# A transformer block in fp32 on one core: the stages of the first phase reordered, the gate stores moved to another DMA queue, and six homes in place of four for the adaLN tiles

## The chip, the cores and the metric

The kernel runs on one core of a Trainium2 chip. Its time is the device time of one execution, in microseconds. The engines are named as the profile names them: PE (matrix multiply, with its weight loads as PEld), DVE (vector), ACT (scalar), POOL (idle here) and SP, which only issues DMAs.

## The reference

One block of batch 1, 256 tokens and width 2048, all in float32. With `mod = silu(c) @ w_ada + b_ada`, cut into nine rows of 2048 (`sh1, sc1, gt1, ... gt3`):

```python
u = modulate(rmsnorm(h, g1), sh1, sc1)
h = h + 0.5 * gt1 * ((silu(u @ w_in_a) * (u @ w_in_b)) @ w_out)      # 2048 -> 2 x 5632 -> 2048
u = modulate(rmsnorm(h, g2), sh2, sc2)
h = h + gt2 * hybrid_mixer(u)     # one wide projection, windowed attention, mLSTM, gates, w_out
u = modulate(rmsnorm(h, g3), sh3, sc3)
h = h + 0.5 * gt3 * swiglu(u, ffn2)
out = rmsnorm(h, final_g)
```

## The kernel before

**Products.** Each fp32 product is made of three in fp32r: ACT rounds a weight block to `hi` (L1452), DVE subtracts to get `lo` (L2040), and PE adds act_hi\*hi, act_lo\*hi and act_hi\*lo. A *chunk* is 1 MB of weights (128x2048); it has two *units*. A unit is 12 matmuls of 512 columns. `raw` holds four chunks and `hi` four units, so SP may load chunk n only when PE is through with chunk n-4, and ACT may round unit n only when PE is through with unit n-4. All engines run their instructions in program order.

**adaLN.** `w_ada` (laid out as 144 blocks of 128 x 2048) is not multiplied on PE. DVE multiplies its tiles by `cond_row` and sums them, one after another. At the start these are 32 *start tiles* of 1 MB (L2069, `start_tile`): tiles 2kt and 2kt+1 give scale and shift of the 128 features kt, without which neither `act_hi` (L1709) nor `act_lo` (L2090) of that kt exists. Later they are tiles of 0.5 MB (L2057, `ada`), which land in a ring of four homes in `ada_w`. The tiles of the attention phase ("gates") have two homes of their own in `gate_w`. `ada_plan` says with which chunk a tile is loaded and used. SP waits for the last tile in a home to be used before it loads the next one there, and everything behind that on SP waits too.

**The first phase** (`first_body`, 36 chunks, 72 units counted from 0) runs the first FFN's input product before all of kt is known. The list `STAGES` sets which kt of which column blocks come in which order. One stage uses the four pairs of PSUM banks `pa, pb` and `px, pq`; when the next stage needs other column blocks, ACT copies the sums out to `part` (L1719) and, where the new block had been begun, copies them back (L1722). `MOVES` lists these copies; `todo` says in which unit ACT issues them. `tile_unit(k)` says before which unit DVE handles start tile k, `load_before(k)` before which chunk SP loads it.

**Gate rows.** `store_gate` (L680) writes a row of `mod` (gt1, gt2, gt3) from SBUF to DRAM as 2048 single elements of 4 bytes; `load_gate` (L686) reads it back broadcast over the partitions. All DMAs but five small ones are issued by SP, on queue q1. The five of ACT go on queue q10.

**After the first phase** come, for each FFN, three input phases (`ffn1_in0..2`) and three output phases (`ffn1_out0..2`). Between them lie `proj`, `rest` (4 chunks of 264 columns) and `gates` (with the attention and mLSTM heads), and `up` and `wout`. Before an output phase can end its first block, the last hidden block has to be multiplied (DVE L2185), turned (DVE L2171, ACT L1463) and split (ACT L1486, DVE L2178).

Of the kernel before, what the change touches and what calls it, by code (L numbers as in the profile page):

```python
# [33 lines left out]
P = 128  # L34
NC = 512
RING = 4
ADA_RING = 4
# [10 lines left out]


GROUPS = 6  # L50
STAGES = [(0, ((0,), (1,))), (1, ((0, 1),)), (2, ((0, 1),)),
# [3 lines left out]
LEFT = range(12, 16)  # L55
# [26 lines left out]
def build(nc, x, x_t, c, cols, positions, w_ada, w_first, ffn1_w_in, ffn1_w_out, w_proj, w_rest, w_gates,  # L82
# [3 lines left out]
    KD = D // P  # L86
# [93 lines left out]
    for cidx in sorted(tiles_at):  # L180
        for t in tiles_at[cidx]:
            load_at.setdefault(cidx + (AHEAD if t in gates_tiles else 0), []).append(t)
    ring_of = {}
    for ring in (gates_tiles, [t for t in range(len(TILES)) if t not in gates_tiles]):
        size = 2 if ring is gates_tiles else ADA_RING
        for k, t in enumerate(ring):
            ring_of[t] = (ring is gates_tiles, k % size, k // size, ring[k - size] if k >= size else None)

    MODS = [(GT1, 3)] + [(m, 1) for m in (SH2, SC2, GT2, SH3, SC3, GT3)]

# [22 lines left out]

    def tile_unit(k):

        return (0, 0, 1, 2)[k] if k < 4 else 3 + round(2.2 * (k - 4))

    def load_before(k):

        return k // 2 if k < 4 else tile_unit(k) // 2 + 1  # L220

    def hi_unit(kt):

# [78 lines left out]
    with ExitStack() as ctx:  # L302
# [356 lines left out]
        def _(sp):  # L659
# [14 lines left out]
                    sp.wait_ge(s_dve, k - S_RING + 1)  # L674
                sp.dma_start(start_home(k), w_ada[m * KD + kt, :, :]).then_inc(ada_s_in[k % S_RING], 16)

            def store_gate(m, done):

                sp.wait_ge(mod_ok, mod_count(m))
                sp.dma_start(gate_rows[ROWS_OUT.index(m):ROWS_OUT.index(m) + 1, :].rearrange("a (k p) -> p (a k)", p=P),  # L680
                             mod[:, m * KD:(m + 1) * KD], allow_slow_non_contiguous=True).then_inc(done, 16)

            def load_gate(row, done, landed):

                sp.wait_ge(done, 16)
# [70 lines left out]

            def load_x_again(b):

                sp.wait_ge(s_dve, 2 * KD)
                if b > 1:  # L760
                    sp.wait_ge(gated_sum, 2 * b - 2)
                sp.dma_start(gate_w[:, b % 2, :].rearrange("p (t n) -> p t n", t=TT), x[:, :, b * NC:(b + 1) * NC])\
                    .then_inc(x_again[b % 2], 16)

            def load_ffn(f):
                g0 = 0
                for p, ng in enumerate(PARTS):
                    name = f"ffn{f}_in{p}"
                    def ffn_in(i, first, name=name, g0=g0):
                        if name == "ffn1_in2" and i == 0:  # L770
                            for k in (0, 1):
                                load_x_again(k)
                        if name in PARTIAL and i < PARTIAL[name][1]:
                            for j in range(plan[name].per[i]):
                                pos = N_FIRST + 2 * (PARTIAL[name][0] + i) + j
                                load(plan[name], i, j, w_first[pos], 4)
                                load_ada(plan[name].at(i) + j)
                            return
                        if (name, i) in FAST:
                            load_fast(name, i)  # L780
                            return
                        for j in range(8):
                            if not at_seam(plan[name], i, j):
                                ffn_chunk(name, i, i + g0, j, j)
                            load_ada(plan[name].at(i) + j)
                            if name == "ffn1_in2" and (i, j) in ((1, 4), (1, 7)):
                                load_x_again(2 + (j == 7))
                            if (name, i, j) == ("ffn1_in1", 3, 3):
                                store_gate(GT1, gt1_out)
                            if (name, i, j) == ("ffn2_in0", 0, 4):  # L790
                                load_pair(0, 0)
                                load_pair(0, 1)
                            if (name, i, j) == ("ffn2_in0", 0, 7):
                                store_gate(GT3, gt3_out)
                    over(sp, ng, ffn_in)
                    name = f"ffn{f}_out{p}"
                    def ffn_out(b, first, name=name, g0=g0, ng=ng):
# [29 lines left out]
                over(sp, 4, body)  # L827

            proj_pair("proj", w_proj)
            store_gate(GT2, gt2_out)  # L830
            for j in range(4):
                load(plan["rest"], 0, j, w_rest[:, j * 4:j * 4 + 4, :], 4, REST_W)
            proj_pair("gates", w_gates)
# [596 lines left out]
        def _(act):  # L1430
# [273 lines left out]
            def first_body(ph):  # L1704
# [18 lines left out]

                todo = {}
                for k, move in enumerate(MOVES):
                    todo.setdefault(move[0] + 3, []).append(k)
                assert [k for u in sorted(todo) for k in todo[u]] == list(range(len(MOVES)))
                for u in range(N_UNITS):
                    split(ph, 0, u // 2, u % 2, 2)
# [27 lines left out]
            def partial_body(ph, i, g, last):  # L1757
# [16 lines left out]
                if last:  # L1774
                    silu(ph)(i)
                    nat_evac_at(nb - 1, i - 1)

            def rows_load(k):

                if k == 0:  # L1780
# [21 lines left out]

            def first_casts(n_):

                if n_ == 10:
                    s_casts("ffn2_in0")
                if n_ >= 12:
                    fast_cast(0, n_ - 12)

            def ffn(f, mid):  # L1810
                for p, ng in enumerate(PARTS):
                    ph = plan[f"ffn{f}_in{p}"]
                    for i in range(ng):
# [4 lines left out]
                        if (f"ffn{f}_in{p}", i) in FAST:  # L1818
                            fast_body(f"ffn{f}_in{p}", i)
                            continue  # L1820
                        in_body(ph, i, i == 0, silu(ph), None, True, mid=mid if p == 0 else None,
                                step=rows_load if (f, p, i) == (1, 2, 0) else
                                first_casts if (f, p, i) == (2, 0, 0) else None)
                        if (f, p, i) == (1, 2, 2):

# [53 lines left out]
            for n_, (j, half, k0, n) in enumerate(units(4, 4)):  # L1879
# [5 lines left out]
                    act.activation(m_st[:, 8:10, :], m_st[:, 10:12, :], ACT.Ln, bias=1.0).then_inc(g_ln, 1)  # L1885
                if n_ == 3:
                    copy_b(3)

            def qk_silu(hds):

# [1150 lines left out]
```

## Time and profile before

| | us |
|---|---|
| median of 3 runs (2038.3 to 2039.84) | 2039.84 |
| the profiled execution's own time | 2043.58 |
| its span, first to last instruction | 2041.8 |
| PE busy | 2019.9 |
| DVE busy | 1685.4 |
| ACT busy | 1206.6 |
| mean granted TensorE clock | 0.997 |

The chain that ended last is 93% PE. The profiled execution lies 3.7 us above the median, and 1.8 us of its time lie outside the span. A group of rows below shows a start time in us from the first instruction, a duration in us, engine, line, operation, names, shape and count, and in brackets the idle time of the engine just before and what ended it.

### The profile page before, as it was taken

To read this page: it belongs to the slowest core of one execution; us is meant where nothing else is said; L and a number is where in the kernel's file an instruction comes from. 1 tells how busy PE (TensorE), PEld (TensorE's weight loads), DVE (VectorE), ACT (ScalarE), POOL (GpSimd) and SP (SyncE) were. 2 spreads that over 40 slices of the span, in tenths; PEclk is the share of its full clock that TensorE was granted. 3 is DMA by queue.
4 is the path that set the end of the run, shared out by engine and by line. 5 is a ranking of instruction groups with operands and counts; after the bars stand their busy time and mean duration, and the time that the engine had idled before them with its cause. 6 is when DMAs were issued, how large, how long until landed. Compare 5 with 4: busy or idle time off the path is not lost.

```text
span 2041.8 us, 23814 instructions
## 1 busy us (share of the span) xinstructions
PE 2019.9 (99%) x9090; PEld 1662.6 (81%) x9090; DVE 1685.4 (83%) x2208; ACT 1206.6 (59%) x1658; POOL 2.4 (0%) x14
## 2 busy tenths in 40 slices
PE   8999999999999999999999999999999999999998
PEld 6788888887888888888777888888888888888887
DVE  7898698878889988788998898887777777787786
ACT  5777644655345555446555676567775577755764
POOL 0000000000000000000000000000000000000000
PEclk8999999999999999999999999999999999999999
DMA  9998799899999868976665687575565556555554
GB/s 386 393 380 310 286 346 385 329 310 372 364 357 345 311 244 347 343 278 182 221 219 209 237 304 270 184 234 179 206 229 204 192 179 210 209 199 201 173 198 150
DMA packets 102658, 544.96 MB, mean 267 GB/s; under 512 B 17424, under 2 KB 19728, under 8 KB 53776
## 3 DMA queue, kind: packets, MB, share of 16 engines
q1 hardware_dynamic: 101696, 543.30, 73.1%
q8 instruction: 72, 1.18, 0.2%
q14 instruction: 42, 0.34, 0.1%
q10 hardware_dynamic: 848, 0.14, 0.0%
HBM read 541.28 MB, written 2.12 MB: 266 GB/s over the span
## 4 chain that ended last, share of the span: by engine, by line
PE 93%; DMA 3%; DVE 2%; ACT 1%; issue 1%; SPq 0%; DVEq 0%; ACTq 0%
PE pa L934 13%; PE pb L934 13%; PE pa L942 13%; PE pb L942 12%; PE pb L938 12%; PE pa L938 12%; DMA raw<-in_ffn_w_in_dram 2%; PE pa L1028 2%; PE pa L1034 2%; PE pa L1031 2%; DMA raw<-in_w_first_dram 1%; PE pa L949 1%; PE pq L1201 1%; PE pa L1192 1%; PE pb L1201 1%; PE pa L1197 1%
## 5 line engine op out<-in xcount | busy, mean ns | idle before, releaser
L1452 ACT CAST hi<-raw 128x1024 fp32r<-128x1024 f32 (+2 forms) x662 | 679.1, 1034 | 694.9 <-PE pa L942 251.5
L2040 DVE TENSOR_TENSOR lo<-raw,hi 128x1024 fp32r<-128x1024 f32 (+2 forms) x662 | 784.6, 1201 | 277.3 <-ACT hi L1452 274.3
L2057 DVE SCALAR_TENSOR_TENSOR ada_w<-ada_w,cond_row 128x1024 f32<-128x1024 f32 x207 | 247.2, 1218 | 0.0
L934 PE MATMUL pa<-hi,act_hi 128*128 128x512 f32 x800 | 222.0, 393 | 0.0
L934 PE MATMUL pb<-hi,act_hi 128*128 128x512 f32 x800 | 217.1, 393 | 0.1
L942 PE MATMUL pb<-lo,act_hi 128*128 128x512 f32 x800 | 213.9, 389 | 0.0
L942 PE MATMUL pa<-lo,act_hi 128*128 128x512 f32 x784 | 213.6, 389 | 0.0
L938 PE MATMUL pb<-hi,act_lo 128*128 128x512 f32 x784 | 209.8, 389 | 0.0
L938 PE MATMUL pa<-hi,act_lo 128*128 128x512 f32 x720 | 196.0, 389 | 0.0
L942 PEld LDWEIGHTS pb<-lo,act_hi 128*128 128x128 f32 x800 | 150.2, 188 | 31.4
L934 PEld LDWEIGHTS pb<-hi,act_hi 128*128 128x128 f32 x800 | 148.6, 188 | 32.4 <-issue 2.2
L934 PEld LDWEIGHTS pa<-hi,act_hi 128*128 128x128 f32 x800 | 148.6, 188 | 31.8 <-issue 1.7
L938 PEld LDWEIGHTS pb<-hi,act_lo 128*128 128x128 f32 x784 | 147.2, 188 | 30.9
L942 PEld LDWEIGHTS pa<-lo,act_hi 128*128 128x128 f32 x784 | 147.2, 188 | 30.8
L938 PEld LDWEIGHTS pa<-hi,act_lo 128*128 128x128 f32 x720 | 135.2, 188 | 28.6
L1463 ACT COPY hid_t<-buf_a 32x256 f32<-32x256 f32 x240 | 97.0, 404 | 15.2 <-DVE buf_a L2171 11.9
L934 PE MATMUL pa<-hi,hid_hi 128*128 128x512 f32 x376 | 103.8, 391 | 1.6 <-ACT hi L1452 1.6
L942 PE MATMUL pa<-lo,hid_hi 128*128 128x512 f32 x376 | 103.3, 390 | 1.1 <-DVE lo L2040 1.1
L938 PE MATMUL pa<-hi,hid_lo 128*128 128x512 f32 x376 | 103.3, 390 | 0.0
L942 PE MATMUL pb<-lo,hid_hi 128*128 128x512 f32 x372 | 102.5, 388 | 0.0
L934 PE MATMUL pb<-hi,hid_hi 128*128 128x512 f32 x330 | 89.2, 389 | 0.0
L938 PE MATMUL pb<-hi,hid_lo 128*128 128x512 f32 x330 | 89.1, 389 | 0.0
(462 smaller groups left out, 2612.5 us busy)
## 6 DMA issues: line engine op xcount, KB each, us to landing
raw<-in_ffn_w_in_dram SPq DMA_DIRECT2D x107, 1024.0 KB, 5.1
ada_w<-in_w_ada_dram SPq DMA_DIRECT2D x207, 512.0 KB, 6.5
raw<-in_ffn_w_out_dram SPq DMA_DIRECT2D x60, 1024.0 KB, 6.8
raw<-in_w_first_dram SPq DMA_DIRECT2D x48, 1024.0 KB, 6.9
raw<-in_w_gates_dram SPq DMA_DIRECT2D x32, 1024.0 KB, 4.9
raw<-in_w_proj_dram SPq DMA_DIRECT2D x31, 1024.0 KB, 5.7
pair<-in_ffn_w_in_dram SPq DMA_DIRECT2D x20, 1024.0 KB, 6.9
raw<-in_ffn_w_out_dram SPq DMA_DIRECT2D x24, 768.0 KB, 4.6
```

Of the source, the lines that this page charges most:

```text
L934: pe.matmul(bank[:, tt, cols], a_hi[:, k0 + kk, tok], w_hi[:, kk, cols], start=start and kk == 0, stop=False, skip_group_check=on)
L938: pe.matmul(bank[:, tt, cols], a_lo[:, k0 + kk, tok], w_hi[:, kk, cols], start=False, stop=False, skip_group_check=on)
L942: mm = pe.matmul(bank[:, tt, cols], a_hi[:, k0 + kk, tok], w_lo[:, 2 * half + kk, cols], start=False, stop=stop and rest is None and kk == ...
L949: mm = pe.matmul(bank[:, tt, cols], a_lo[:, k0 + kk, tok], w_hi[:, kk, cols], start=False, stop=stop and kk == n - 1, skip_group_check=on)
L1028: pe.matmul(bank, a_hi[:, kk, :], fast_hi(o)[:, kk, :], start=start and kk == 0, stop=False, skip_group_check=True)
L1031: pe.matmul(bank, a_lo[:, kk, :], fast_hi(o)[:, kk, :], start=False, stop=False, skip_group_check=True)
L1034: mm = pe.matmul(bank, a_hi[:, kk, :], fast_lo(o)[:, kk, :], start=False, stop=kk == 1, skip_group_check=True)
L1201: mm = pe.matmul(bank(m)[:, tt, :], act_hi[:, blocks[m][0], tok], w_lo[:, s0 + m, 0:NC], start=False, stop=True, skip_group_check=True)
L1452: act.copy(hi_of(ph, i, j, half)[:, 0:n, 0:w], raw_of(ph, i, j)[:, 2 * half:2 * half + n, 0:w])\
L1463: ins = act.copy(dst, src)
L2040: dve.tensor_tensor(lo_of(ph, i, j)[:, s, 0:w], raw_of(ph, i, j)[:, s, 0:w], hi_of(ph, i, j, half)[:, 0:n, 0:w].bitcast(F32), ALU.subtract)\
L2057: dve.scalar_tensor_tensor(out=wt, in0=wt, scalar=1.0, in1=cond_row[:, half * ADA_W:(half + 1) * ADA_W], op0=ALU.mult, op1=ALU.mult, accum ...
```

## The change

Three parts. (1) In the first phase the first stage has kt 0 alone, its second stage kt 0 and then kt 1, and the sixth kt 1, 2 and 3; start tiles are handled up to two units later and loaded up to one chunk later, and ACT copies the banks of the first stage out one unit after their last use, not three. (2) The three stores of a gate row go from SP's queue to ACT's, each at a later place of the program. (3) The adaLN tiles up to the third block of `ffn1_out1` take turns in six homes: the four of `ada_w` and the two of `gate_w`. The reloads of x into `gate_w` wait for the last of them.

```diff
-STAGES = [(0, ((0,), (1,))), (1, ((0, 1),)), (2, ((0, 1),)),
-          (2, ((2,), (3,))), (1, ((2, 3),)), (0, ((2, 3),)),
+STAGES = [(0, ((0,),)), (1, ((0,), (1,))), (2, ((0, 1),)),
+          (2, ((2,), (3,))), (1, ((2, 3),)), (0, ((1, 2, 3),)),
...
+    WIDE = [t for cidx in tiles_at for t in tiles_at[cidx] if cidx < plan["ffn1_out1"].at(2) + 2]
+    ring_of, holder, turns = {}, {}, [0] * (ADA_RING + 2)
+    for ring, first_slot, size in ((WIDE, 0, ADA_RING + 2),
+                                   ([t for t in range(len(TILES)) if t not in WIDE + gates_tiles], 0, ADA_RING),
+                                   (gates_tiles, ADA_RING, 2)):
...
     def tile_unit(k):
-        return (0, 0, 1, 2)[k] if k < 4 else 3 + round(2.2 * (k - 4))
+        return (0, 0, 2, 4)[k] if k < 4 else 5 + round(2.2 * (k - 4))
     def load_before(k):
-        return k // 2 if k < 4 else tile_unit(k) // 2 + 1
+        return (0, 0, 1, 2)[k] if k < 4 else tile_unit(k) // 2 + 1
...
             def load_x_again(b):
-                sp.wait_ge(s_dve, 2 * KD)
+                sp.wait_ge(ada_done, LAST_WIDE[b % 2] + 1)
...
-                            if (name, i, j) == ("ffn1_in1", 3, 3):
-                                store_gate(GT1, gt1_out)
-                            if (name, i, j) == ("ffn2_in0", 0, 7):
-                                store_gate(GT3, gt3_out)
...
             proj_pair("proj", w_proj)
-            store_gate(GT2, gt2_out)
...
-                    todo.setdefault(move[0] + 3, []).append(k)
+                    todo.setdefault(move[0] + (1 if move[1] == 0 else 3), []).append(k)
...
+            def store_gate(m, done):
+                act.wait_ge(mod_ok, mod_count(m))
+                act.dma_start(gate_rows[ROWS_OUT.index(m):ROWS_OUT.index(m) + 1, :].rearrange("a (k p) -> p (a k)", p=P),
+                              mod[:, m * KD:(m + 1) * KD], allow_slow_non_contiguous=True).then_inc(done, 16)
+            def first_gate(n_):
+                if n_ == 8:
+                    store_gate(GT1, gt1_out)
...
             def first_casts(n_):
+                if n_ == 8:
+                    store_gate(GT3, gt3_out)
...
+                if n_ == 5:
+                    store_gate(GT2, gt2_out)
```

The first place is the start of the first phase. ACT's rows from its first rounding on, before (`act_hi` is the split input of one kt, `part<-pa` a bank copied out):

```order
L1452 CAST hi<-raw 128x1024
L1709 ACTIVATE act_hi<-n_t,mod 128x256
L1452 CAST hi<-raw 128x1024 x2
L1709 ACTIVATE act_hi<-n_t,mod 128x256
L1452 CAST hi<-raw 128x1024 x3
L1719 COPY part<-pa 128x1024
L1719 COPY part<-pb 128x1024
```

and now (L1447, L1704 and L1714 are L1452, L1709 and L1719 of before):

```order
L1447 CAST hi<-raw 128x1024
L1704 ACTIVATE act_hi<-n_t,mod 128x256
L1447 CAST hi<-raw 128x1024
L1714 COPY part<-pa 128x1024
L1714 COPY part<-pb 128x1024
L1447 CAST hi<-raw 128x1024
L1714 COPY part<-px 128x1024
L1714 COPY part<-pq 128x1024
L1447 CAST hi<-raw 128x1024 x2
L1704 ACTIVATE act_hi<-n_t,mod 128x256
```

Two pairs of copies now stand before and behind the rounding of unit 2, and the second `act_hi` comes behind unit 4 in place of unit 2. DVE's rows there, from the first `act_lo` on, before (`ada_s`, `ada_w` <- ... are start tiles 2 and 3):

```order
L2090 SCALAR_TENSOR_TENSOR act_lo<-n_t,mod,act_hi 128x256
L2040 TENSOR_TENSOR lo<-raw,hi 128x1024
L2069 SCALAR_TENSOR_TENSOR ada_s,macc<-ada_s,cond_row 128x2048
L2040 TENSOR_TENSOR lo<-raw,hi 128x1024
L2069 SCALAR_TENSOR_TENSOR ada_w,macc<-ada_w,cond_row 128x2048
L2076 TENSOR_TENSOR mod<-macc,cols_in 128x1
L2077 SCALAR_TENSOR_TENSOR gain<-macc,sc_bias,cols_in 128x1
L2084 SCALAR_TENSOR_TENSOR n_t<-n_t,gain,rs_row 128x256
L2090 SCALAR_TENSOR_TENSOR act_lo<-n_t,mod,act_hi 128x256
L2040 TENSOR_TENSOR lo<-raw,hi 128x1024
```

and now (L2051, L2080 and L2101 are L2040, L2069 and L2090 of before):

```order
L2101 SCALAR_TENSOR_TENSOR act_lo<-n_t,mod,act_hi 128x256
L2051 TENSOR_TENSOR lo<-raw,hi 128x1024 x2
L2080 SCALAR_TENSOR_TENSOR ada_s,macc<-ada_s,cond_row 128x2048
L2051 TENSOR_TENSOR lo<-raw,hi 128x1024 x2
L2080 SCALAR_TENSOR_TENSOR ada_w,macc<-ada_w,cond_row 128x2048
L2087 TENSOR_TENSOR mod<-macc,cols_in 128x1
L2088 SCALAR_TENSOR_TENSOR gain<-macc,sc_bias,cols_in 128x1
L2095 SCALAR_TENSOR_TENSOR n_t<-n_t,gain,rs_row 128x256
L2101 SCALAR_TENSOR_TENSOR act_lo<-n_t,mod,act_hi 128x256
L2051 TENSOR_TENSOR lo<-raw,hi 128x1024
```

Start tile 2 has moved behind the `lo` of unit 1, and tile 3, with what makes kt 1 of it, behind the `lo` of unit 3. SP's loads there, before:

```order
L675 DMA ada_s<-in_w_ada_dram 128x2048 x2
L700 DMA raw<-in_w_first_dram 128x2048
L675 DMA ada_s<-in_w_ada_dram 128x2048
L675 DMA ada_w<-in_w_ada_dram 128x2048
L700 DMA raw<-in_w_first_dram 128x2048
L742 DMA n_t<-in_x_t_dram 128x512
L675 DMA ada_w<-in_w_ada_dram 128x2048
L700 DMA raw<-in_w_first_dram 128x2048
L675 DMA gate_w<-in_w_ada_dram 128x2048
```

and now:

```order
L681 DMA ada_s<-in_w_ada_dram 128x2048 x2
L700 DMA raw<-in_w_first_dram 128x2048
L681 DMA ada_s<-in_w_ada_dram 128x2048
L700 DMA raw<-in_w_first_dram 128x2048
L681 DMA ada_w<-in_w_ada_dram 128x2048
L700 DMA raw<-in_w_first_dram 128x2048
L742 DMA n_t<-in_x_t_dram 128x512
L681 DMA ada_w<-in_w_ada_dram 128x2048
L700 DMA raw<-in_w_first_dram 128x2048
```

The second and the third chunk of `raw` now each have one tile less ahead of them. The second place is the store of gt2. SP's rows before, at the end of `proj`:

```order
L668 DMA ada_w<-in_w_ada_dram 128x1024 [waits ada_done] x2
L700 DMA raw<-in_w_proj_dram 128x2048 [waits unit_used] x3
L680 DMA gate_rows<-mod 128x16x1 [waits mod_ok]
L700 DMA raw<-in_w_rest_dram 128x4x264 [waits unit_used] x4
L700 DMA raw<-in_w_gates_dram 128x2048 [waits unit_used] x4
```

and ACT's now, in `rest`:

```order
L1894 ACTIVATE m_st<-m_st 128x8
L1447 CAST hi<-raw 128x2x264 x2
L1861 ACTIVATE proj<-pb 128x2x512
L1447 CAST hi<-raw 128x2x264 x2
L1776 DMA gate_rows<-mod 128x16x1
L1447 CAST hi<-raw 128x2x264 x2
L1907 ACT_TABLE_LOAD
L1907 ACTIVATE proj<-proj,cols_in 128x2x128 x4
L1447 CAST hi<-raw 128x1024
```

The store no longer stands ahead of the loads of `rest` on SP; it stands on ACT behind the rounding of the sixth unit of `rest`, when SP has come to the loads of `gates`.

## Rows read from the trace of the kernel before

**Rows 1.** The page, busy time and instructions of the engines.

```profile
PE 2019.9 (99%) x9090; PEld 1662.6 (81%) x9090; DVE 1685.4 (83%) x2208; ACT 1206.6 (59%) x1658; POOL 2.4 (0%) x14
```

**Rows 2.** Windows (stretch: length, busy by engine, clock, DMA share, GB/s).

```profile
20.00:40.00 20.00, 17.05 (x62) 13.22 (x61) 18.70 (x22) 9.19 (x11) 0.00 (x0) 0.83 1.01 423
```

**Rows 3.** Timeline of PE, start of the first phase.

```profile
12.37 0.71 PE L1171 MATMUL pq<-ident,st 128*128 128x128 f32 x4 [2.70 <-DVE st L2606]
...
19.48 0.70 PE L1192 MATMUL pa<-hi,act_hi 128*128 128x512 f32 x2 [0.38 <-ACT act_hi L1709]
...
28.41 1.19 PE L1192 MATMUL pa<-hi,act_hi 128*128 128x512 f32 x2 [2.83 <-ACT act_hi L1709]
...
33.66 0.93 PE L1192 MATMUL px<-hi,act_hi 128*128 128x512 f32 x2
...
36.73 1.07 PE L1192 MATMUL pa<-hi,act_hi 128*128 128x512 f32 x4
...
39.45 1.07 PE L1192 MATMUL pb<-hi,act_hi 128*128 128x512 f32 x4
```

**Rows 4.** Timeline of PE, units 20 and 24 of the first phase.

```profile
80.25 1.16 PE L1192 MATMUL pa<-hi,act_hi 128*128 128x512 f32 x4
...
92.99 0.40 PE L1192 MATMUL pa<-hi,act_hi 128*128 128x512 f32 x1
```

**Rows 5.** Timeline of ACT, start of the first phase.

```profile
26.81 1.04 ACT L1452 CAST hi<-raw 128x1024 fp32r<-128x1024 f32 x1 [6.53 <-DMA raw<-in_w_first_dram]
27.76 0.50 ACT L1709 ACTIVATE act_hi<-n_t,mod 128x256 fp32r<-128x256 f32 x1
...
34.29 1.00 ACT L1719 COPY part<-pa 128x1024 f32<-128x1024 f32 x1
```

**Rows 6.** Timeline of DVE, start tile 3 and what follows.

```profile
24.25 2.28 DVE L2069 SCALAR_TENSOR_TENSOR ada_w<-ada_w,cond_row 128x2048 f32<-128x2048 f32 x1
...
26.90 0.48 DVE L2084 SCALAR_TENSOR_TENSOR n_t<-n_t,gain,rs_row 128x256 f32<-128x256 f32 x1
```

**Rows 7.** Windows behind two gate stores, and beside four small loads of ACT.

```profile
432.50:441.00 8.50, 8.50 (x39) 7.02 (x39) 5.88 (x10) 3.58 (x6) 0.00 (x0) 1.00 0.67 43
918.00:928.00 10.00, 10.00 (x48) 8.30 (x47) 8.93 (x17) 3.91 (x5) 0.00 (x0) 1.00 0.46 18
558.00:568.00 10.00, 10.00 (x46) 8.29 (x45) 9.66 (x13) 4.01 (x4) 0.00 (x0) 1.00 0.98 381
```

**Rows 8.** The line of the gate stores, L680.

```profile
DMA to landing us min/median/max: 15.4/15.9/16.0
```

**Rows 9.** Timelines of ACT and PE, start of `ffn1_out1`.

```profile
469.49 2.00 ACT L1452 CAST hi<-raw 128x1024 fp32r<-128x1024 f32 x2 [2.90 <-DMA raw<-in_ffn_w_out_dram]
...
475.86 3.33 ACT L1463 COPY hid_t<-buf_a 32x256 f32<-32x256 f32 x8 [1.62 <-DVE buf_a L2171]
...
485.89 1.17 PE L934 MATMUL pa<-hi,hid_hi 128*128 128x512 f32 x4 [1.57 <-ACT hi L1452]
...
489.09 1.19 PE L942 MATMUL pa<-lo,hid_hi 128*128 128x512 f32 x4 [1.11 <-DVE lo L2040]
```

**Rows 10.** Timelines of ACT and PE, second block of `ffn2_in0`.

```profile
1373.16 2.00 ACT L1452 CAST hi<-raw 128x1024 fp32r<-128x1024 f32 x2 [5.38 <-DMA raw<-in_ffn_w_in_dram]
...
1379.42 0.73 PE L1028 MATMUL pa<-hi_b,s_in 128*128 128x512 f32 x2 [1.36 <-ACT pa L1521]
```

**Rows 11.** Timelines of ACT and PE, end of `rest`, start of `gates`.

```profile
938.28 0.64 ACT L1452 CAST hi<-raw 128x528 fp32r<-128x528 f32 x1 [0.20 <-PE px L942]
...
944.72 1.03 ACT L1452 CAST hi<-raw 128x1024 fp32r<-128x1024 f32 x1
...
948.38 1.07 PE L934 MATMUL pa<-hi,act_hi 128*128 128x512 f32 x4
...
954.75 1.07 PE L934 MATMUL pa<-hi,act_hi 128*128 128x512 f32 x4
```

**Rows 12.** Waits of SP's queue (total us, times, longest).

```profile
SPq L668 <- DVE ada_w L2057: 279.1, 113, 9.5
```

More of the change, by code:

```diff
@@ L182, in build @@
             load_at.setdefault(cidx + (AHEAD if t in gates_tiles else 0), []).append(t)
-    ring_of = {}
-    for ring in (gates_tiles, [t for t in range(len(TILES)) if t not in gates_tiles]):
-        size = 2 if ring is gates_tiles else ADA_RING
-        for k, t in enumerate(ring):
-            ring_of[t] = (ring is gates_tiles, k % size, k // size, ring[k - size] if k >= size else None)
+    WIDE = [t for cidx in tiles_at for t in tiles_at[cidx] if cidx < plan["ffn1_out1"].at(2) + 2]
[3 more added lines that the diff above has]
+                                   (gates_tiles, ADA_RING, 2)):
+        for k, t in enumerate(ring):
+            s = first_slot + k % size
+            ring_of[t] = (s >= ADA_RING, s % ADA_RING, turns[s], holder.get(s))
+            turns[s] += 1
+            holder[s] = t
+    LAST_WIDE = [max(t for t in WIDE if ring_of[t][:2] == (True, s)) for s in (0, 1)]
     MODS = [(GT1, 3)] + [(m, 1) for m in (SH2, SC2, GT2, SH3, SC3, GT3)]
@@ L675, in load_start @@
                 sp.dma_start(start_home(k), w_ada[m * KD + kt, :, :]).then_inc(ada_s_in[k % S_RING], 16)
[L677 to L681, printed above, removed]
             def load_gate(row, done, landed):
@@ L1822, in ffn @@
                                 step=rows_load if (f, p, i) == (1, 2, 0) else
+                                first_gate if (f, p, i) == (1, 1, 3) else
                                 first_casts if (f, p, i) == (2, 0, 0) else None)
```

## The prediction

> **What bounds the kernel now.** First the page: PE is busy for 2019.9 of 2041.8 us [rows 1]. So a change can only win where PE stands still, runs at its lower clock, or takes its operands as they come. I read the timeline of PE for these places and found four that the change can reach. All else that PE loses (some 10 us before its first product at 19.48, the small products of the heads) is not touched.
>
> (a) Start. A unit takes 39.45 - 36.73 = 2.72 us, at full clock and with all its operands there [rows 3]. PE begins unit 0 at 19.48 and unit 4 at 36.73. Four units cost 10.88 us, so 6.37 us are lost. 2.83 of them are idle time ahead of unit 2. Most of the rest is clock: unit 2 takes 33.66 - 28.41 = 5.25 us, and the window 20:40 has a mean clock of 0.83 [rows 2, 3].
> (b) Units 20 to 23 take 92.99 - 80.25 = 12.74 us in place of 10.88: 1.86 us lost, behind ACT's copies of banks [rows 4].
> (c) `ffn1_out1`: 1.57 and 1.11 us at 485.89 and 489.09 [rows 9].
> (d) `ffn2_in0`: 1.36 us at 1379.42 [rows 10].
>
> Together 6.4 + 1.9 + 2.7 + 1.4 = 12.4 us. That is the ceiling.
>
> **The start, step by step.** Before, unit 2 needs kt 1: the rounding of its chunk, at 26.81 as the DMA lands, then `act_hi` at 27.76, then PE at 28.41 [rows 3, 5]. DVE would have been no sooner: start tile 3 from 24.25, its `n_t` ready at 27.38 [rows 6]. Now units 2 and 3 need only kt 0, and their banks must first be copied out.
>
> Unit 1: 22.3 to 25.0 (19.48 + 2.81 with the first one's fill). ACT copies `pa` and `pb` from 22.5, when unit 0 is through, for 1.0 us each [rows 5], so until 24.4. The second chunk has 1 MB less ahead of it in SP's queue; 1 MB at 423 GB/s [rows 2] is 2.5 us, so it lands at 24.3 in place of 26.8. Rounding until 25.4. Unit 2 runs 25.5 to 28.2: idle 0.5. Then ACT copies `px` and `pq` (to 27.3) and rounds (to 28.3). Unit 3 runs 28.4 to 31.1: idle 0.2.
>
> Unit 4 needs kt 1. DVE subtracts unit 3 (28.3 to 29.5) and only then takes tile 3. From a tile's start to the end of `n_t` it is 27.38 - 24.25 = 3.13 us [rows 6]: 32.6. `act_hi` 33.1, PE 33.3. Idle 2.2 us. So unit 4 starts 36.73 - 33.3 = 3.4 us earlier, if the clock stays up.
>
> After that DVE takes tile 4 before the `lo` of unit 5: 34.8 + 2.3 + 1.2 = 38.3, wanted at 36.0 + 1.8 = 37.8. That loses 0.5. I followed the units to 12, and `act_hi` of kt 2 and 3 and their chunks come in time, the closest by some 0.5 us. In (b) the burst of copies is the same, moved two units ahead, but with one `act_hi` less inside it. ACT gains 0.4 us, DVE's tile then comes 0.8 us late for one unit. I take 1.0 us lost in place of 1.86. Sum at full clock: 3.4 - 0.5 + 0.9 = 3.8 us won.
>
> The clock: idle stretches of 2.70 and 2.83 us were followed by the lower level of 1.2 GHz [rows 2, 3]; the one of 1.57 us in (c) was not: the matmuls after it keep their pace [rows 9]. 2.2 us lies between, nearer to those that fell. The cost of a fall is at most what it is now, 5.25 - 2.72 = 2.5 us and 0.4 us of unit 3; with less idle time I take 1.7. A slow unit 4 hides the 0.5 of unit 5. So 3.8 - 1.7 + 0.5 = **2.6 us**; between 1.0 (full cost) and 3.8 (no fall).
>
> **The gate stores.** Each is issued in 0.43 us and lands 15.4 to 16.0 us later [rows 8]. Behind it the core's DMA nearly stops: 43 GB/s from 432.5 to 441, 18 from 918 to 928 [rows 7], and the third the same behind 1360. Some 3 MB, 8 to 9 us of the queue. What hangs on it: in (d) ACT waited 5.38 us for a chunk until 1373.16, rounds four units in a row, and so copies `pa` late [rows 10]. In (c) ACT is still at 469.49 bound to a chunk as it lands; DVE's product of the last hidden block stands behind the `lo` of that chunk, the turning waits until 475.86, 16 copies and a split follow, and the next rounding is late [rows 9].
>
> From ACT's queue there are two bounds. The upper one: four small loads of ACT, 768 elements or rows in all, passed beside SP's loads from 558 to 568 at 381 GB/s for both, with no dent [rows 7]. If the store goes the same way while SP's queue is full, its elements slip in one by one. The lower: nothing gained, only the place changes. I expect something between: it slips in while SP's queue is full, and what is left blocks as soon as the queue runs empty.
>
> The Trainium skill, DMA: Bandwidth & Descriptors, section "Issuing engines are not separate DMA queues", says that DMAs of all engines end on the same 16 DMA engines and that another issuer saves only issue time. By that rule the move would win nothing in itself; (c) and (d) would then change only by the store's new place. No row before shows a store on ACT's queue.
>
> (c): the store is issued some 16 us later, at about 441 of the old time. The chunks of the last block then still have 8 us of slack (a chunk is issued four chunks ahead, 16 us before its unit). The SP queue is also freed: of its 279 us of waits for adaLN homes, each up to 9.5 us [rows 12], those of this phase fall with six homes. The chunk that lands at 469.5 should land 3 us earlier, which is more than the 2.68 us of both waits. I take **2.7**; 0 to 2.7.
> (d): ACT issues at about 1351, 3 us earlier than SP did, while SP's queue is full. A part slips in, the stop behind it is shorter, the chunk lands 2 to 3 us earlier; the copy needs 1.4. I take **1.0**; 0 to 1.4.
>
> **Six homes** elsewhere: they hide behind a busy PE. DMAs keep their order, so no chunk lands later for it. The x reloads wait for tiles used long before. Worth 0 outside (c). Two or three more DMA issues on ACT: 0.4 us each, in front of a rounding that is units ahead: 0.
>
> **What can get worse: gates.** The store of gt2 now is issued at 938.9, behind the cast of 938.28 [rows 11], while chunks of `gates` are about to be read. If they lie behind it, they land with or after it: 938.9 + 15.9 = 954.8 [rows 8], 2.5 us later with their own MB, plus 1.05 for the rounding. The second chunk is wanted at 954.75 [rows 11]: 1.1 to 3.6 us lost. The first is rounded at 944.72 and could wait for 2.6 us, being wanted at 948.38. I take **0.5 us** lost, since it will be in flight by then.
>
> **Sum.** 2.6 + 2.7 + 1.0 - 0.5 = 5.8 us. Span: 2041.8 - 5.8 = 2036.0. Time of a profiled execution: 2043.58 - 5.8 = 2037.8; the median lies 3.7 lower: 2034.0.
>
> **Rivals.**
> - *Only a part* (the clock falls for its full cost, or one of (c) and (d) stays): 1.0 + 2.7, 2.6 + 1.0 or so, less 0.5: 2.5 to 4 won, 2036 to 2037.5. For it: the 2.2 us of idle time, and the skill's rule on the queues. Chance 0.27.
> - *Slower*: the gates. If the first chunk of `gates` also lies behind the store, PE waits 954.8 + 1.05 - 948.4 = 7.5 us, and the fall of the clock after it costs 2.9. That is 10.4 against 2.6 + 2.7 + 1.0: 2044. It decides once the chunk lands more than 2.6 + 6.3 = 9 us later than now. Against it: the chunk is issued 0.6 us ahead of the store. Chance 0.10.
> - *Nothing to be seen*: kt 1 as late as before. It would take the second chunk at 26.8 as now and a full fall of the clock, and the stores blocking (c) from their new place: 2039 to 2040. Chance 0.05.
> - *The forecast*, 2031.9 (all at their best, 3.8 + 2.7 + 1.4, and nothing lost in gates) to 2036: 0.58.
>
> A measurement of this kernel tells about 0.2%, 4.1 us, from no change: faster means below 2035.8. All the forecast up to there and a bit of the part case: 0.60. Same: 0.29. Slower: 0.11. Range: 2030.5, below the best sum by the spread of the runs, to 2040.0, which leaves out the slower rival and something of the others.
>
> **What would show it.** Timeline of PE: unit 2 at 25.5, unit 4 near 33.3 behind about 2.2 us of idle time; window 20:40 at a clock of 0.9 or more. No idle time before the seventh unit of `ffn1_out1` and before the product of 1379. The line of the stores with landings over 16 us where SP's queue is full, and no window of 9 us under 100 GB/s. Wrong it would be if the second chunk still lands at 26.8, if PE waits at the start of `gates` for a chunk, or if a new wait of SP for `gt1_out` holds back loads behind it.

## The result, and the profile after

The changed kernel takes 2048.97 us (median of 5 runs, 2047.08 to 2050.3) against 2039.84 of before: ratio 1.0046, 95% interval 1.0031 to 1.006, some 9 us slower. The forecast was 2034.0, faster, with a range from 2030.5 to 2040.0. The profiled execution took 2050.23 us, its span is 2048.5.

The page's first lines after, and below them windows: the start, and the stretches behind the three gate stores (columns as in [rows 2]).

```profile
PE 2023.7 (99%) x9090; PEld 1666.3 (81%) x9090; DVE 1685.6 (82%) x2208; ACT 1207.5 (59%) x1658; POOL 2.4 (0%) x14
```

```profile
34.00:40.00 6.00, 6.00 (x21) 4.75 (x21) 6.00 (x6) 4.17 (x6) 0.00 (x0) 0.72 1.02 426
438.50:449.00 10.50, 10.50 (x48) 8.71 (x47) 7.02 (x9) 5.79 (x10) 0.00 (x0) 1.00 1.03 79
941.00:951.00 10.00, 10.00 (x68) 9.21 (x67) 6.17 (x16) 8.13 (x16) 0.00 (x0) 1.00 1.10 55
1369.00:1374.00 5.00, 5.00 (x24) 4.14 (x23) 5.00 (x6) 5.00 (x7) 0.00 (x0) 1.00 0.91 50
```

PE's busy time grew by 3.8 us with the same 9090 products: that is clock, not work. The stops of the DMA [rows 7] are still there, only elsewhere. PE's timeline at its waits after:

```profile
25.56 0.73 PE L1187 MATMUL pa<-hi,act_hi 128*128 128x512 f32 x2 [0.24 <-ACT hi L1447]
...
33.28 0.71 PE L1187 MATMUL pa<-hi,act_hi 128*128 128x512 f32 x2 [1.93 <-ACT act_hi L1704]
...
484.31 1.56 PE L929 MATMUL pa<-hi,hid_hi 128*128 128x512 f32 x4 [2.58 <-ACT hi L1447]
485.67 1.91 PE L933 MATMUL pa<-hi,hid_lo 128*128 128x512 f32 x4
...
955.40 1.66 PE L929 MATMUL pa<-hi,act_hi 128*128 128x512 f32 x4 [1.83 <-ACT hi L1447]
956.85 1.91 PE L933 MATMUL pa<-hi,act_lo 128*128 128x512 f32 x4
...
967.16 0.88 PE L1369 MATMUL pq<-ident,w_sb 128*128 128x128 f32 x3 [3.33 <-DVE m_st L2815]
967.68 2.06 PE L929 MATMUL pa<-hi,act_hi 128*128 128x512 f32 x4
969.54 1.91 PE L933 MATMUL pa<-hi,act_lo 128*128 128x512 f32 x4
```

The first two rows answer to [rows 3]: units 2 and 4 start where the forecast had them (25.5 and 33.3). The third is (c) [rows 9]: one wait of 2.58 us in place of two of 1.57 and 1.11, and now the lower clock behind it, where four products of 512 columns take 1.91 us in place of 1.07. The product of [rows 10] has no wait now. Two places are new, at the start of `gates` [rows 11], and the lower clock follows each of them too. In the queues of SP and ACT there (SP's row merges four issues; the line in the second block is of the landings of the first two):

```profile
936.93 9.70 SPq L700 DMA_DIRECT2D raw<-in_w_gates_dram  x4
```

```profile
DMA to landing us min/median/max: 7.8/11.1/14.5
```

```profile
936.95 0.41 ACTq L1776 DMA_DIRECT2D gate_rows<-mod  x1
...
954.30 2.00 ACT L1447 CAST hi<-raw 128x1024 fp32r<-128x1024 f32 x2 [3.88 <-DMA raw<-in_w_gates_dram]
```

SP issues four chunks of `gates` from 936.93 on, ACT the store at 936.95; the second chunk, issued at 939.8, lands 14.5 us after its issue (5.0 before), and ACT, which has waited for it, rounds it at 954.30. PE wanted it at 953.4: it starts four products of 512 columns every 0.91 us here, and the last four ahead of this chunk's start at 952.50.

The landings of the three gate stores (L1776) after:

```profile
DMA to landing us min/median/max: 15.6/17.8/22.6
```

gt2's is the 15.6, gt3's the 17.8 and gt1's the 22.6.

### The profile page after: what moved, and what is told of

Its sections match the earlier page's. It is cut to its first block, busy times and chain, and to the rows that moved or that the text cites. A ratio compares the mean times of both kernels' runs of the same rounds, so it can differ in the third digit from the quotient of the medians.

```text
span 2048.5 us, 23810 instructions
## 1 busy us (share of the span) xinstructions
PE 2023.7 (99%) x9090; PEld 1666.3 (81%) x9090; DVE 1685.6 (82%) x2208; ACT 1207.5 (59%) x1658; POOL 2.4 (0%) x14
## 4 chain that ended last, share of the span: by engine, by line
PE 94%; DMA 2%; DVE 2%; ACT 1%; issue 0%; SPq 0%; DVEq 0%; ACTq 0%
PE pa L929 13%; PE pb L929 13%; PE pa L937 13%; PE pb L937 13%; PE pb L933 12%; PE pa L933 12%; PE pa L1029 2%; PE pa L1023 2%; PE pa L1026 2%; PE pa L944 1%; PE pb L1196 1%; DMA raw<-in_ffn_w_in_dram 1%; PE pa L1187 1%; PE px L1187 1%; PE px L1196 1%; PE pq L1196 1%
## 5 line engine op out<-in xcount | busy, mean ns | idle before, releaser
L1447 ACT CAST hi<-raw 128x1024 fp32r<-128x1024 f32 (+2 forms) x662 | 680.2, 1035 | 686.3 <-PE pa L937 282.5
L2051 DVE TENSOR_TENSOR lo<-raw,hi 128x1024 fp32r<-128x1024 f32 (+2 forms) x662 | 784.8, 1201 | 282.2 <-ACT hi L1447 279.0
L2068 DVE SCALAR_TENSOR_TENSOR ada_w<-ada_w,cond_row 128x1024 f32<-128x1024 f32 x179 | 214.1, 1218 | 0.0
L1458 ACT COPY hid_t<-buf_a 32x256 f32<-32x256 f32 x240 | 96.9, 404 | 15.4 <-DVE buf_a L2182 12.0
```

The costliest lines, as they stand in the source:

```text
L1447: act.copy(hi_of(ph, i, j, half)[:, 0:n, 0:w], raw_of(ph, i, j)[:, 2 * half:2 * half + n, 0:w])\
L1458: ins = act.copy(dst, src)
L2051: dve.tensor_tensor(lo_of(ph, i, j)[:, s, 0:w], raw_of(ph, i, j)[:, s, 0:w], hi_of(ph, i, j, half)[:, 0:n, 0:w].bitcast(F32), ALU.subtract)\
L2068: dve.scalar_tensor_tensor(out=wt, in0=wt, scalar=1.0, in1=cond_row[:, half * ADA_W:(half + 1) * ADA_W], op0=ALU.mult, op1=ALU.mult, accum ...
```

## The experiments

All times are medians; the ratio is to runs of before on the same chip. The medians of before were 2039.0, 2039.1, 2041.5 and 2040.2 in the four groups of runs, so kernels of different groups are compared by ratio. A lead of 1 us in the table below that only kernels of different groups show can be of that size too.

For places the traces are compared product by product (each has 9090 products on PE): the start of the same product in the kernel before, second execution, less that in the kernel. Positive is ahead of before. (c) lies between the columns 477.3 and 490.4, the start of `gates` between 941.9 and 964.2, and (d) behind 964.2.

```
product at, us of before:    98.7   477.3   490.4   941.9   964.2   end
before, first execution      -1.5    -1.9    -3.4    -3.8    -3.8   -5.1
changed kernel                1.2     1.2    -2.2    -2.5   -12.2  -11.7
x1_start                      1.3     1.3     1.4     1.2     1.1    0.8
x2_stores                     0.9     0.9    -1.6    -1.5    -9.6   -9.2
x3_homes                     -0.3    -0.4     0.0    -0.1    -0.1    0.2
x4_gt2sp                      1.5     1.5    -1.4    -1.5    -1.5   -1.0
x5_allsp                      1.4     1.3     1.3     1.1     1.1    0.5
x6_before_turned             -0.4    -0.4     1.2     1.4     1.4    1.9
x7_after_turned               1.0     1.0     2.6     2.4     2.4    3.0
x8_sp_turned                  2.5     2.5     4.0     3.8     3.8    4.4
x9_sp_newplace                2.8     2.8    -0.2    -0.5   -10.8  -10.3
x10_act_oldplace              1.1     0.8    -2.5    -2.8    -2.8   -2.5
x11_tile3                     4.3     4.3     5.9     5.8     5.8    6.2
x12_half                      2.5     2.5    -0.2    -0.5    -9.8   -9.2
x13_512                       1.2     1.2    -2.2    -2.2    -8.4   -7.8
x14_128                       1.2     1.2    -1.8    -1.9    -6.7   -6.1
x15_best4                     4.0     4.0     5.6     5.3     5.3    5.6
```

**The parts apart.** `x1_start` is before with part 1 alone, `x2_stores` with part 2 alone, `x3_homes` with part 3 alone.

> The kernel before with part 1 alone (stages, start tiles, copies one unit after use); stores on SP's queue, four homes. Theory A (the loss of the change is the store of gt2 in front of the chunks of gates, and nothing in part 1): the changed kernel was 3.0 us ahead of before at 446 us, and loads, stores and waits of this kernel hang on PE's progress, so the 3.0 us stay to the end: 2036.8. Rival B (the DMA is saturated up to ffn1_out1, so its chunks land at the same absolute time and the lead is given back there): at 490 us a lead of at most 1.5 us is left, 2038.3. Rival C (part 1 itself loses somewhere later): 2040 or more.

> The kernel before with part 2 alone (the three gate stores on ACT's queue at their new places). Theory A: gates loses some 9.4 us, which is what the lead of the changed kernel fell by between 490 and 964 us; ffn2_in0 wins 1.4; ffn1_out1, whose chain ended 1.6 us earlier in the changed kernel, wins 1.6 to 2.7: in all 5.5 us slower, 2045.3. Rival B (six homes or the start brought the loss of gates): 2036 to 2038, with no wait of PE at the start of gates.

> The kernel before with part 3 alone (six homes up to the third block of ffn1_out1, x reloads waiting for their last use). Theory A: the waits of SP for homes fall, but PE is not fed by them: 2039.8, within 0.5 us. Rival B (the 1.6 us by which ffn1_out1's chain ended earlier in the changed kernel come from the homes, not from the store): 2038.2. Rival C (two more tiles in flight delay the chunks behind them where the DMA is saturated): 2040.5 or more, with longer waits at 486 us.

Measured: part 1 2037.42, ratio 0.9991 (0.9982 to 0.9999), some 1.8 us faster and not 3.0. Part 2 2048.57, 1.0046 (1.0033 to 1.0058): the whole loss. Part 3 2038.45, 0.9997 (0.9988 to 1.0006): nothing. The table has part 2's loss at two places, 2.5 us at `ffn1_out1` and 8.0 in `gates`; theory A had a gain at the first and was wrong there. Then each store was put back:

```diff
 x4_gt2sp: the changed kernel (gt2's store leaves ACT)
             proj_pair("proj", w_proj)
+            store_gate(GT2, gt2_out)
...
 x5_allsp: that, and (the other two leave ACT)
+                            if (name, i, j) == ("ffn1_in1", 3, 3):
+                                store_gate(GT1, gt1_out)
+                            if (name, i, j) == ("ffn2_in0", 0, 7):
+                                store_gate(GT3, gt3_out)
```

> The changed kernel with the store of gt2 alone put back on SP's queue between proj and rest. Theory A: the 9.4 us lost in gates are gone: by the medians 2049.0 - 9.4 = 2039.6, by the traces (a lead of 1.2 us at 490, plus 1.4 in ffn2_in0) 2.6 us below before, 2037.2. Rival B (a store on ACT's queue or the homes cost elsewhere): above 2041.

> The changed kernel with all three stores back on SP's queue at the places of before: parts 1 and 3 alone. Theory A (gt1's store at its new place, not the homes, makes ffn1_out1 wait 2.7 us at once and brings the clock's fall there): at most 1.3 us of waiting at ffn1_out1, 1.5 us faster than with gt1's and gt3's stores moved (2038.7 against 2039.0 of before), so 1.5 to 2 below the runs of before. Rival B (the six homes do it): 2.7 us at ffn1_out1, no better than -0.4 against before.

`x4_gt2sp` 2038.66, 0.9999 (0.999 to 1.0008): the loss of `gates` is gone. `x5_allsp` 2037.97, 0.999 (0.998 to 0.9999), and between 477 and 490 it loses nothing against before where `x4_gt2sp` loses 2.9 us. PE's timeline at `ffn1_out1` in `x5_allsp`:

```profile
481.22 1.15 PE L940 MATMUL pa<-hi,hid_hi 128*128 128x512 f32 x4 [0.17 <-ACT hi L1458]
...
484.40 1.19 PE L948 MATMUL pa<-lo,hid_hi 128*128 128x512 f32 x4 [1.13 <-DVE lo L2046]
```

So moving gt1's store costs at (c), and the homes do not: both kernels have six. The two kernels differ in the store's place and queue at once, so for gt1 these are not taken apart; and gt3's store moves with it, but only later, near 1350.

**Before, once more.**

> The kernel before, once more, one execution with its trace. Two kernels that touch neither place had no idle time or 1.3 us at the start of ffn1_out1, and 0.7 or none in ffn2_in0, where the profiled execution of before lost 2.68 and 1.36. Theory A: these waits belong to that one execution (its stores took 15.4 to 16.0 us, those of the others 13.8 to 14.9) and not to the median: this one takes 2038.5 to 2040 with less than 2 us lost in the two places together. Rival B: they are before's own, and the two kernels removed them: 3.5 to 4.5 us lost here as well.

2038.48 us, span 2036.7. PE's timeline has one wait of (c), and the window of the start the full clock, where [rows 3] had the lower one (0.50 from 28 to 34):

```profile
28.70 0.70 PE L1192 MATMUL pa<-hi,act_hi 128*128 128x512 f32 x2 [2.49 <-ACT act_hi L1709]
...
485.68 1.20 PE L942 MATMUL pa<-lo,hid_hi 128*128 128x512 f32 x4 [1.10 <-DVE lo L2040]
```

```profile
28.00:34.00 6.00, 5.17 (x22) 4.02 (x23) 5.42 (x7) 3.37 (x5) 0.00 (x0) 1.00 1.01 426
```

The stores land in 13.7 to 14.3 us here, in 15.4 to 16.0 in [rows 8]. The wait of (d) is 0.30 us. The span of this execution is 5.1 us shorter than the one the forecast was read from: 1.6 at the start (clock), 1.5 at `ffn1_out1`, 0.4 between, 1.0 in `ffn2_in0`, and 0.6 in small things. Theory A holds for (c): PE waits 1.1 us there, with some 0.2 more ahead of it, and `x1_start`, `x3_homes` and `x5_allsp`, with this store at its old place, have one wait of 1.05 to 1.13 us as well. The wait of (d) varies: 1.36 and 0.30 us in the two executions of before, 0.55, none and 0.91 in these three kernels.

**Queue or place.** gt2's store in the changed kernel, on SP's queue at the new place, and on ACT's queue near the old one:

```diff
 x9_sp_newplace (SP; gt2's store leaves ACT)
...
+                        if (name, i, j) == ("gates", 0, 0):
+                            store_gate(GT2, gt2_out)
...
 x10_act_oldplace (ACT; the store leaves its step in rest)
...
             def proj_step(n_):
+                if n_ == 14:
+                    store_gate(GT2, gt2_out)
```

> The changed kernel with the store of gt2 on SP's queue, between the loads of chunk 0 and chunk 1 of gates, at the time at which ACT issued it. Theory A (the place costs, not the queue): chunk 1 of gates lands 13 us or more after its issue, PE waits for its rounding, 8 to 10 us slower than with the store at the end of proj: 2047 to 2049. Rival B (ACT's queue costs): 2040 or less.

> The changed kernel with the store of gt2 on ACT's queue, but behind the rounding of the 15th unit of proj's last block, near 909 us, when SP issued it before. Theory A (the place costs): as with the store on SP's queue at the end of proj (2038.7), within 1 us. Rival B (ACT's queue costs): 2045 or more.

`x9_sp_newplace` 2050.27, 1.0044 (1.003 to 1.0058), and 10.3 us lost in `gates`; `x10_act_oldplace` 2039.85, 0.9992 (0.9983 to 1.0001), nothing lost there (its store came at 920.4, 11 us later than planned, since ACT reaches that place then, and the DMA moved 18 GB/s for the 12 us from 921 on). For gt2's store the place decides, not the queue.

**What stops the DMA.** The store as 64 runs of 128 bytes in four DMAs, from a tile that DVE turned:

```diff
...
+                    link(dve.tensor_tensor(gate_s[:, row, 0:KD], mod[:, cols_], bada[:, cols_], ALU.add))
+                    dve.transpose(gate_t[:, row, :], gate_s[:, row, :]).then_inc(mod_ok, 1)
...
+                for q in range(4):
+                    sp.dma_start(gate_rows[row, :].rearrange("(k q r) -> q k r", q=4, r=32)[q],
+                                 gate_t[32 * q:32 * q + KD, row, :]).then_inc(done, 16)
```

> The kernel before, each store at its old place on SP's queue but of 64 runs of 128 bytes in four DMAs: DVE writes the gate row to a tile of its own and turns it in 32x32 blocks first. Theory A (the stop of the DMA comes from the 2048 elements of 4 bytes): the DMAs land in 3 to 7 us, no microsecond behind them is under 100 GB/s, PE has no wait at ffn1_out1 and ffn2_in0; by the median it wins what the median still loses there, 0 to 2 us: 2038. Rival B (the stop comes from any small write into DRAM, whatever its count): a stop of 5 us or more is still there, 2039 or more.

> The changed kernel with the same turned stores, on ACT's queue at the changed places. Theory A: the 9.4 us of gates and the 3.5 of ffn1_out1 are gone with the stop: the start's 3.2 us below the median of before and up to 1 more, 2035.5. Rival B (a store on ACT's queue in front of the chunks of gates costs by its place, whatever its size): PE still waits over 1 us at the start of gates, 2040 or more.

> As the last one, but with the four DMAs of each turned store on SP's queue at the places of before. Theory A (the queue does not matter once the elements are few): 2035.5, within 1 us of the last one. Rival B (SP's four issues of 0.4 us each in front of loads, or ACT's in front of roundings, cost): the two differ by over 1.5 us.

`x6_before_turned` 2036.58, 0.9987 (0.9978 to 0.9995); `x7_after_turned` 2034.29, 0.9977 (0.9968 to 0.9986); `x8_sp_turned` 2034.27, 0.9978 (0.9968 to 0.9988). None of the three waits at `ffn1_out1`. The line of the four DMAs of each store, and the stretches behind them, in `x8_sp_turned`:

```profile
DMA to landing us min/median/max: 3.9/5.2/5.8
```

```profile
421.00:431.00 10.00, 10.00 (x46) 8.29 (x45) 9.67 (x14) 5.78 (x10) 0.00 (x0) 1.00 0.93 355
906.00:916.00 10.00, 10.00 (x49) 8.30 (x48) 8.86 (x16) 5.88 (x7) 0.00 (x0) 1.00 0.50 161
```

355 GB/s where before had 156 from 428 to 438, and 161 against 18. (At the second place some of the low rate is not the store's: in this kernel too single microseconds pass there without traffic, though its stores have landed.) The better comparison is `x7_after_turned` with the changed kernel, the same places on the same queue, 325 and 298 GB/s in place of 79 and 55:

```profile
436.00:446.00 10.00, 10.00 (x46) 8.28 (x45) 7.47 (x9) 7.33 (x13) 0.00 (x0) 1.00 0.89 325
932.00:942.00 10.00, 10.00 (x82) 9.87 (x82) 7.05 (x15) 8.04 (x15) 0.00 (x0) 1.00 0.86 298
```

With turned stores the two queues are equal. Then I divided the store of gt2 in the changed kernel: 1024, 1536 or 1920 of its 2048 elements go at the end of `proj` on SP, the rest on ACT at the changed place (in `x12_half` columns 8 to 15 of 16, in `x13_512` the last four, in `x14_128` the last one).

> The changed kernel with the store of gt2 in two halves of 1024 elements: the first on SP's queue at the end of proj, the second on ACT's queue at the changed place. Theory A (the stop grows with the elements, and the 9 us come of one chunk that passes its due time by some 3 us): the stop behind ACT's half is 3 to 5 us, chunk 1 of gates lands near 950 and PE loses at most 1 us there: 2038 to 2040. Rival B (the stop has a fixed length for any such store): 2046 or more.

> The changed kernel with gt2's store cut 12 to 4: twelve of its 16 columns (1536 elements of 4 bytes) on SP's queue at the end of proj, four (512 elements) on ACT's queue at the changed place. Theory A (the stop has a fixed length for any such store): some 8 us under 100 GB/s behind the second one too, 2047 to 2050. Rival B (there is a number of elements between 512 and 1024 below which it is shorter): a stop of under 5 us, below 2043.

> As the last one, cut 15 to 1: 1920 elements at the end of proj, 128 elements of 4 bytes (one for each partition) on ACT's queue at the changed place. Theory A (a fixed length): some 8 us under 100 GB/s behind them, 2047 to 2050. Rival B: no stop, no wait of PE in gates, 2038 to 2040.

`x12_half` 2049.66, 1.0042 (1.0027 to 1.0057); `x13_512` 2046.26 and `x14_128` 2044.61, one execution each beside runs of before of 2040.2. The windows behind the second part, of the three kernels in this order:

```profile
940.00:950.00 10.00, 10.00 (x64) 9.04 (x63) 5.81 (x12) 7.18 (x15) 0.00 (x0) 1.00 0.93 57
```

```profile
941.00:949.00 8.00, 5.93 (x46) 5.41 (x44) 3.16 (x10) 2.23 (x6) 0.00 (x0) 1.00 0.99 63
```

```profile
940.00:947.00 7.00, 6.60 (x51) 6.09 (x50) 3.83 (x11) 3.02 (x6) 0.00 (x0) 1.00 1.10 62
```

Some 60 GB/s for 10, 8 and 7 us behind 1024, 512 and 128 elements, 55 for 10 us behind 2048. `x5_allsp`, with no store there, moves 324 GB/s from 940 to 947. My theory that the stop grows in step with the elements fell: a sixteenth of them still stops the DMA for 7 us. The turned store differs from this in three things at once, the length of a run (128 bytes for 4), the number of runs (64 for 128 and more) and their layout. Which of them does it was not taken apart: no run has 64 single elements, or single elements laid out otherwise. Why the chip does this no run here tells.

**The start.** With turned stores, start tile 3 goes ahead of the subtraction of unit 3 on DVE (`x11_tile3`); `x15_best4` is the same with four homes.

```diff
-        return (0, 0, 2, 4)[k] if k < 4 else 5 + round(2.2 * (k - 4))
+        return (0, 0, 2, 3)[k] if k < 4 else 5 + round(2.2 * (k - 4))
-        return min(NEW[kt], tile_unit(2 * kt + 1) + (0 if kt < 2 else 4), N_UNITS - 2)
+        return min(NEW[kt], tile_unit(2 * kt + 1) + (0, 1, 4)[min(kt, 2)], N_UNITS - 2)
```

> The kernel of turned stores on SP's queue, with start tile 3 ahead of the subtraction of unit 3 on DVE instead of behind it. Worked out from its trace (unit 3 at 28.37, tile 3 landed at 26.19, subtraction of unit 2 done at 26.61): n_t of kt 1 at 29.7 in place of 32.5, subtraction of unit 3 until 30.9, so PE waits 0.7 us in unit 3 and unit 4 starts at 31.9 in place of 33.2; chunk 3 still comes in time. Theory A: 1.3 us faster, and more where the clock fell behind the idle time of 1.9: 2033.0. Rival B (the chunks, which land at the same time, or the next tile take the gain back): 2034.3.

> The kernel before with part 1, turned stores at the old places on SP's queue, and start tile 3 ahead of the subtraction of unit 3: the fastest kernel so far without the six homes. Theory A (the homes are worth nothing): 2032.4, as with six homes, or a ratio to before of 0.996. Rival B (with four homes SP's waits for a home hold back chunks now that nothing else does): 1 us or more slower than with six.

`x11_tile3` 2032.35 (2032.35 to 2032.6), 0.9956 (0.9944 to 0.9969): the fastest kernel here, 9 us below the runs of before beside it. `x15_best4` 2032.84, 0.9962 (0.9949 to 0.9975): the homes are worth nothing there either. PE's timeline in `x11_tile3`:

```profile
30.84 0.73 PE L1211 MATMUL px<-lo,act_hi 128*128 128x512 f32 x2 [0.54 <-DVE lo L2050]
...
31.87 0.62 PE L1202 MATMUL pa<-hi,act_hi 128*128 128x512 f32 x2
```

The idle time of 1.9 us has become 0.54, and unit 4 starts at 31.87, as worked out.

## Why the prediction was wrong, by its steps

The terms of the sum beside what the traces have, in us won by the changed kernel in each stretch, against both executions of before:

| stretch | forecast | first execution | second execution |
|---|---|---|---|
| start, to 98.7 | 2.6 | 2.8 | 1.2 |
| 98.7 to 477.3 | 0 | 0.3 | -0.1 |
| (c), 477.3 to 490.4 | 2.7 | -1.9 | -3.4 |
| 490.4 to 941.9 | 0 | 0.1 | -0.3 |
| `gates`, 941.9 to 964.2 | -0.5 | -9.7 | -9.7 |
| (d), 964.2 to the end | 1.0 | 1.7 | 0.5 |
| sum | 5.8 | -6.7 | -11.7 |

The second execution lies nearer to the median of before (2038.48 against 2039.84, the first 2043.58). Two steps failed: the price of the gates, and the sign of (c). PE's wait at the start of `gates` was also one of the signs that the prediction named for being wrong.

**The start: right in its times, its size set by the clock.** Unit 2 at 25.56 (25.5), unit 3 at 28.44 (28.4), unit 4 at 33.28 behind 1.93 us (33.3 behind 2.2), units 20 to 23 in 11.72 us, with 0.8 us of loss left (1.0). Against the first execution of before, from which the forecast was read, the changed kernel is 2.8 us ahead at 98.7, against the second 1.2. The reason is the clock: before fell to the lower level (0.50 from 28 to 34) in one execution and not in the other; the changed kernel fell in part (0.72 from 34 to 40), as `x1_start` did (0.76, behind 1.92 us of waiting), and `x8_sp_turned`, with the same 1.92 us, did not (1.00) and is 2.5 ahead. The other length of idle time shows the same: behind 2.49 us `x6_before_turned` has 0.72 from 28 to 34, the second execution of before 1.00. By the ratio part 1 is worth 1.8 us; I took 2.6, within 1.0 to 3.8.

**(c) and (d): the wrong ground.** The step "the median lies 3.7 lower: 2034.0" takes the waits of the first execution, 2.7 + 1.4 us, off a median that has most likely less of them: the second execution has 0.2 + 1.1 us at (c) and 0.3 at (d). Of the 5.1 us between the two spans 2.5 are lost in these two places and 1.6 by the clock at the start. The gap of 3.7 us between profile and median, which I wrote down, was taken off a second time, beside the waits and the fall of the clock that it at least in part consists of.

**(c): the sign.** "The chunk that lands at 469.5 should land 3 us earlier" failed. It landed at 467.9, 1.6 earlier, while PE was 3.1 us ahead of the first execution at 477: the gain of the start moved the due time as well. And the store's stop lay from 438.5 to 449 in place of 432.5 to 441, 6 to 8 us later, and longer than the 8 us of slack that I gave the chunks behind it. Forecast 2.7 won; measured 1.9 lost against the first execution and 3.4 against the second, with 2.58 of waiting and the clock behind it. The moved stores make 2.9 of it: `x4_gt2sp`, with gt1's store moved, falls back by 2.9 us there, and `x5_allsp`, with it back, by 0.1.

**(d): right.** No wait there; 1.7 us won between 964 and the end against the first execution and 0.5 against the second (1.0 forecast). None of the kernels with gt3's store on ACT's queue or turned waits there.

**Six homes: right**, nothing, in `x3_homes` and `x15_best4`.

**The stores: half right.** gt3's store came as forecast: issued at 1356.8, it left the DMA at 415 GB/s from 1357 to 1365, landed after 17.8 us, and its stop of under 100 GB/s is 5 us (1369 to 1374), where it was 11 (1359 to 1370) and, in the second execution, 8 (1356 to 1364). In the packets of the trace some 280 of its 2048 elements went out up to 1365, among SP's, and the rest in the 6 us behind. gt1's and gt2's stores stopped the DMA for 10 us as before, though gt1's took 22.6 us to land. What made gt3's different, the fill of SP's queue or something else, no run takes apart. The rule of the Trainium skill that I cited (DMA: Bandwidth & Descriptors, "Issuing engines are not separate DMA queues": the same 16 DMA engines, whoever issues) is what the runs bear out for gt2's store: ratio 0.9999 on SP's queue and 0.9992 on ACT's at the old place of gt2, 1.0044 and 1.0046 at the new.

**Gates: the step that failed.** "I take 0.5 us lost, since it will be in flight by then." That holds for the first chunk only, and barely: issued 0.02 us ahead of the store, it landed at 944.73, and PE did not wait for it. The second was issued 2.9 us behind the store, and its own bound in the same paragraph was 1.1 to 3.6 us lost; the 0.5 lies below it without a reason. The bound was right: the chunk landed 17.3 us behind the issue of the store (15.9 to 18.4 forecast), and PE lost 2.0. That the clock time is nearly that of the forecast, 954.28 for 954.8, is luck, since the store was issued 1.95 us earlier than forecast. What I left out makes up the rest of the 9.7 us, read product by product: 2.0 wait, 1.7 clock behind it, 3.5 at the heads, 2.5 clock again. I had priced the clock only in the rival, and the heads nowhere. They hang on a load that I did not count, an adaLN tile behind the chunks, issued at 946.68 and landing 13.8 us later (5.9 in the second execution of before): of PE's 3.33 us of idle time ahead of the heads' product, DVE spends 2.76 waiting for this tile. DVE's timeline after, and in the second execution of before:

```profile
960.50 1.23 DVE L2068 SCALAR_TENSOR_TENSOR gate_w<-gate_w,cond_row 128x1024 f32<-128x1024 f32 x1 [2.76 <-DMA gate_w<-in_w_ada_dram]
...
966.85 0.16 DVE L2815 TENSOR_SCALAR m_st<-m_st 128x4 f32<-128x4 f32 x1
```

```profile
951.03 1.22 DVE L2057 SCALAR_TENSOR_TENSOR gate_w<-gate_w,cond_row 128x1024 f32<-128x1024 f32 x1
...
957.38 0.16 DVE L2804 TENSOR_SCALAR m_st<-m_st 128x4 f32<-128x4 f32 x1
```

The chain from the tile to the maximum of the scores takes 6.35 us in both; it starts 9.47 us later after, and PE's product of the heads (957.69, 967.16) comes 9.47 us later. The rival "slower" named this store and these chunks and gave 2044, but asked for the first chunk to be late; the second one and the tile were enough. Its chance of 0.10 was too low for a place where my own bounds were 1.1 to 3.6.

## What to carry to other kernels

Where the profiled execution is longer than the median, the waits in it that hang on a landing time may be that execution's own: read a second one before they are booked as gain. In this kernel a DMA with 4-byte elements into DRAM was paid by what was queued within the next 7 to 11 us, from SP's queue as from ACT's, down to 128 elements. Write runs of 128 bytes, as the turned store does, or put it where every load behind it, small ones too, has more slack than that. A term with bounds of its own goes into the sum within them. After a wait of PE of about 2 us, price the lower clock as possible, and follow each in-order engine that a late load stands in front of.

## What the runs showed of the hardware

The length of the DMA's stop hardly falls with the number of 4-byte elements: 10 us at 55 GB/s for 2048, 7 us at 62 GB/s for 128. The queue that issues the store does not matter for it: 74 GB/s from 938 to 948 behind SP's store in `x9_sp_newplace`, 55 from 941 to 951 behind ACT's. The clock may fall or not behind idle time of the same length: 0.72 (`x6_before_turned`) and 1.00 (before, second execution) from 28 to 34 us behind 2.49 us, and 0.76 (`x1_start`) and 1.00 (`x8_sp_turned`) from 34 to 40 behind 1.92 us.
